# Issuing an attention head's turn, the next head's scores and the previous head's weighing between the same two projection blocks

## The reference

```
proj = rmsnorm(x) @ w_in
A: 4 heads, each with two score maps:  p = softmax(q1 k1) - lam * softmax(q2 k2);  out = p @ v   (v 128 wide)
B: a gated mixing over chunks of 128 tokens
C: 8 heads of 64, three dilated windows combined by their log sums;  out = p @ v
x + (sum over branches of sigmoid(gate) * (y_branch @ w_branch)) @ w_out
```

## Time and profile before

| | |
|---|---|
| runs | median 1844.72 us (1844.07 to 1848.36, 3 runs) |
| profiled execution | span 1845.3 us |
| TensorE | busy 96%, 84% of the chain that ended last |
| VectorE, ScalarE, GpSimd | busy 70%, 56%, 1% |
| granted TensorE clock | mean 0.994 |
| first layer's slots 20 to 57 | about 79.7 to 205.6 us of the span |
| second layer's | about 358.5 to 484.5 us |

### The profile page before, as it was taken

How to read it: one execution, slowest core, us unless ns; L and a number is a source line. 1 busy time by engine, 2 the same in 40 slices (tenths; PEclk the granted TensorE clock), 3 DMA queues, 4 the chain that set the end, 5 groups by cost and what they waited for, 6 DMA issues and landing times.

```text
span 1845.3 us, 46473 instructions
## 1 busy us (share of the span) xinstructions
PE 1776.4 (96%) x18048; PEld 1707.5 (93%) x18048; DVE 1291.2 (70%) x2618; ACT 1034.4 (56%) x2049; POOL 23.5 (1%) x20
## 2 busy tenths in 40 slices
PE   7999999999999999999999999999989988899998
PEld 7999999999998999988899999999987877799998
DVE  6788687788686765587566764676558786657764
ACT  7656656656655555556456554555445844255553
POOL 0110000110000000000000000000000000000000
PEclk9999999999999999999999999999999999999999
DMA  7555555555564555533235555555562320036663
GB/s 247 158 190 172 161 194 178 160 161 159 158 193 128 182 180 178 165 120 97 66 98 170 174 176 176 163 178 180 178 212 92 106 79 4 4 115 193 190 189 123
DMA packets 76990, 279.07 MB, mean 151 GB/s; under 512 B 9008, under 2 KB 10416, under 8 KB 76336
## 3 DMA queue, kind: packets, MB, share of 16 engines
q1 hardware_dynamic: 76848, 277.03, 47.4%
HBM read 274.90 MB, written 1.05 MB: 150 GB/s over the span
## 4 chain that ended last, share of the span: by engine, by line
PE 84%; DVE 9%; ACT 4%; issue 2%; DMA 1%; SPq 0%; DVEq 0%; ACTq 0%
PE psum L410 24%; PE psum L411 23%; PE psum L412 23%; DVE weights_low L375 3%; ACT weights_high L367 2%; PE psum L2991 1%; DMA weight_ring<-weights_in 1%; PE psum L733 1%; PE psum L2968 1%; PE psum L754 1%; PE psum L2985 1%; PE psum L562 1%; PE psum L2575 1%; DVE arena L2974 0%; PE psum L745 0%
## 5 line engine op out<-in xcount | busy, mean ns | idle before, releaser
L375 DVE TENSOR_TENSOR weights_low<-weight_ring,weights_high 128x512 fp32r<-128x512 f32 x984 | 666.5, 697 | 413.3 <-ACT weights_high L367 400.2
L367 ACT ACTIVATE weights_high<-weight_ring 128x512 fp32r<-128x512 f32 x984 | 603.5, 628 | 509.0 <-PE psum L412 506.0
L410 PE MATMUL psum<-ffn_normed_high,weights_high 128*128 128x272 f32 x1056 | 303.9, 288 | 3.4 <-DVE weights_low L375 2.1
L412 PE MATMUL psum<-ffn_normed_high,weights_low 128*128 128x272 f32 x1056 | 302.6, 287 | 0.0
L411 PE MATMUL psum<-ffn_normed_low,weights_high 128*128 128x272 f32 x1056 | 302.6, 287 | 0.0
L410 PE MATMUL psum<-first_normed_high,weights_high 128*128 128x256 f32 x1024 | 293.2, 286 | 5.2 <-DVE weights_low L375 4.6
L411 PE MATMUL psum<-first_normed_low,weights_high 128*128 128x256 f32 x1024 | 285.1, 278 | 0.0
L412 PE MATMUL psum<-first_normed_high,weights_low 128*128 128x256 f32 x1024 | 285.1, 278 | 0.0
L410 PEld LDWEIGHTS psum<-first_normed_high,weights_high 128*128 128x128 f32 x1024 | 193.1, 189 | 14.9 <-DVE weights_low L375 7.2
L410 PEld LDWEIGHTS psum<-ffn_normed_high,weights_high 128*128 128x128 f32 x1056 | 198.9, 188 | 5.9 <-issue 5.7
L411 PEld LDWEIGHTS psum<-ffn_normed_low,weights_high 128*128 128x128 f32 x1056 | 198.9, 188 | 0.1
(11 more groups left out here) (490 smaller groups left out, 3726.3 us busy)
## 6 DMA issues: line engine op xcount, KB each, us to landing
weight_ring<-weights_in SPq DMA_DIRECT2D x507, 512.0 KB, 3.5
arena<-first_in SPq DMA_DIRECT2D x1, 2112.0 KB, 11.0
consts<-const_in SPq DMA_DIRECT2D x1, 1895.0 KB, 7.6
arena<-vec_in SPq DMA_DIRECT2D x1, 1536.0 KB, 8.9
arena<-vec_in SPq DMA_DIRECT2D x1, 1152.0 KB, 5.6
residual<-x_in SPq DMA_DIRECT2D x2, 544.0 KB, 5.2
normed<-arena SPq DMA_DIRECT2D x64, 16.0 KB
out<-normed SPq DMA_DIRECT2D x4, 256.0 KB, 2.3
```

Of the source, the lines that this page charges most:

```text
L367: nc.scalar.activation(WH[:, n % SPLIT, half], W[:, n % RING, half], ACT.Copy).then_inc(weights_high, 1)
L375: nc.vector.tensor_tensor(WL[:, n % SPLIT, half], W[:, n % RING, half], WH[:, n % SPLIT, half].bitcast(F32), ALU.subtract).then_inc(weight ...
L410: nc.tensor.matmul(psum, WH[:, s, cols], high, start=start, stop=False)
L412: return nc.tensor.matmul(psum, WL[:, s, cols], high, start=False, stop=stop)
```

## The change

Scores now stand three slots ahead of a head's turn, which is the slot of the turn of the head before it. Weighing stands in the slot of the next head's turn; for the last head it stays one behind. Maximum and taking move with them, the exponential moves to t-2 and normalising to t-1. Within a slot the order on PE is scores, turn, weighing, and on DVE maximum, taking, normalising, as before. No operation is added or left out.

```diff
+        SCORES_AT = {i - 3: head for i, head in HEADS_AT.items()}
+        WEIGH_AT = {i + 3 if i + 3 in HEADS_AT else i + 1: head for i, head in HEADS_AT.items()}
...
-                if i + 4 in HEADS_AT:
-                    head_scores(*HEADS_AT[i + 4])
+                if i in SCORES_AT:
+                    head_scores(*SCORES_AT[i])
                 if i in HEADS_AT:
                     head_turn(*HEADS_AT[i])
-                if i - 1 in HEADS_AT:
-                    head_weigh(*HEADS_AT[i - 1])
+                if i in WEIGH_AT:
+                    head_weigh(*WEIGH_AT[i])
...
-                if i + 3 in HEADS_AT:
-                    kind, h = HEADS_AT[i + 3]
+                if i + 2 in HEADS_AT:
+                    kind, h = HEADS_AT[i + 2]
                     act_exp(act, attn[kind, l], h)
...
-                if i + 4 in HEADS_AT:
-                    kind, h = HEADS_AT[i + 4]
+                if i in SCORES_AT:
+                    kind, h = SCORES_AT[i]
                     dve_masked_max(dve, attn[kind, l], h, mask_c if kind == "C" else mask_a)
-                if i - 1 in HEADS_AT:
-                    kind, h = HEADS_AT[i - 1]
+                if i in WEIGH_AT:
+                    kind, h = WEIGH_AT[i]
                     if kind == "A":
                         dve_take_head(dve, attn[kind, l], h, YS[:, 0:4])
...
-                if i + 2 in HEADS_AT:
-                    kind, h = HEADS_AT[i + 2]
+                if i + 1 in HEADS_AT:
+                    kind, h = HEADS_AT[i + 1]
                     dve_normalise(dve, attn[kind, l], h, NEG_LAM[:, l:l + 1])
```

## The result

The changed kernel takes 1856.37 us (median of 6 runs, 1853.33 to 1859.54) where the kernel before takes 1845.39 beside it (6 runs, 1841.98 to 1850.02): a ratio of 1.0061, with a 95% interval from 1.0047 to 1.0075. It is slower by about 11 us; forecast were 12.

A forecast was written before the change was run, and what follows sets the result against it. TensorE was taken as the bound, with 84% of the chain. Turn stalls of 14.6 us, less 2.3 for block 29's wait and 0.4 for seams, gave +11.9: median 1857 us, 8-in-10 range 1849 to 1862.

The forecast's parts named there:

- DVE's and ACT's lateness: Ahead of head turns: exponentials and normalising, moved one block later, end late, so TensorE stalls 7.30 us per layer.
- the rope pair ahead of C1 and C3: DVE slots 25 and 31: a rope pair of 1.51 us delays normalising, so each turn stalls 0.92 us.
- GpSimd's 0.9 at C1 and 0.7 at C2: DVE's normalising there may meet GpSimd's rope product: 0.9 and 0.7 us more stall, each 0 to 1.3.
- ACT's branch part at A1: Slot 48: ACT's high part of branch C adds 0.94 us of work, so A1's turn stalls 1.03 us.
- The wait at block 29: Behind C2's turn, low weights late on DVE: the whole 1.15 us goes, 2.3 us for two layers.
- Seams: Between small work and projection blocks: scores followed by turns save 0.35 us per layer, net 0.2, or 0.4 in all.
- the 0.15 given back: Slots 19 and 33: scores C0/C1 and weighing C2/C3 lose their company, costing 0.15 us per layer (0 to 0.2).
- Rival 1: Only the large stalls, at C1, C3, A1 and A3, are real: +5.1 us, 1850; chance 0.18.
- Rival 2: DVE's normalising is never late, only block 29's wait and seams count: 1842 or 1841 us; chance 0.07.
- Rival 3: Late turns delay DVE's weight parts, so projection blocks wait too: +17 to +19 us, 1863; chance 0.09.
- Rival 4: TensorE's clock falls to 1.2 GHz for one block at each of 24 turns: +65 us, 1920; chance 0.01.
- clock 1.00: A listed sign of the forecast: TensorE's granted clock stays at 1.00, that is, does not fall.

The follow-up runs named there:

- e2: Changed kernel with weighing and taking put back one slot behind the turn, so only scores, maximum, exponential and normalising move: 1859.14 us, 1.0057 to the kernel before.
- e3: Changed kernel with each turn, and ACT's copy of it, one slot later, restoring the distance from scores to turn: 1848.50 us, 1.0015 to the kernel before.
- e5: Changed kernel with DVE's normalising issued ahead of the rope pair in its slot: 1854.61 us, 1.0056 to the kernel before.
- e7: Changed kernel with GpSimd's cosine product of rope pairs 5 and 6 cut to 8 of 256 columns: 1849.21 us, one run.
- e6: Changed kernel with ACT's high part of branch C in slot 50 instead of 48, DVE's low part in 51 instead of 49: 1858.89 us, one run.
- e1: Kernel before with only weighing and taking moved to the slot of the next head's turn: 1846.67 us, 0.9990 to the kernel before.
- e4: The changed kernel run once more, unaltered: 1856.67 us, 1.0053 to the kernel before.
- e8: Changed kernel with two scratch fills added on DVE ahead of C1's normalising, to lengthen TensorE's wait: 1862.11 us, one run.

## Why the prediction was right, step by step

**DVE's and ACT's lateness.** This was the core of the forecast, and it held: 7.30 per layer forecast, 7.74 and 8.11 measured. The waits view has TensorE waiting in both stretches for nothing but normalising ahead of a turn; e2 puts four fifths of these waits on the moved scores alone (6.45 and 6.18), and e3 shows them gone when the distance is given back. The terms one by one: the rope pair ahead of C1 and C3 (.92 each) is shown by e5 and measured at .95 in e7; GpSimd's 0.9 at C1 and 0.7 at C2 measured 0.95 to 1.05 and 0.7 to 0.9 (e7 against the changed kernel), at C1 by the meeting with normalising that I had forecast, at C2 by one with the weight splits or the rope pair that stand ahead of it, so that term was right in size more than in place; ACT's branch part at A1 is shown by e6, forecast 1.03, measured 0.97 and 1.17; A3 is 0.15 longer than the sum of its parts, A0 and A2 between 0.1 less and 0.1 more. C5 waits for nothing; C7, for which I had nothing too, waits 0.07. The rule of the Trainium skill (SBUF — State Buffer, "SBUF: two separate sides") that the loser at the port pair waits for the whole instruction fits C1's rows: DVE's operation started at 100.14 with 1.20 of the product to run, took 1.48 less 0.42, that is 1.06, longer than elsewhere, and ended 0.28 behind the product. That the cost then stays in the kernel, and only changes the operation that pays, is what e5 adds.

**What was removed.** The wait at block 29 is gone, 1.15 and 1.18 of it, as said.

**Seams.** The net gain was mis-sized. Groups less waits are 22.39 and 22.34 in the changed kernel, and 24.09 and 24.05 less the 1.15 and 1.18 are 22.94 and 22.87 before: 0.55 and 0.53 per layer, with 12 groups fewer, where I took 0.2. Two terms of my sum were off. "0 to 0.1 each", of which I took the middle, 0.35 in all: scores and a turn cost 1.06 and 0.34 apart (last matmul of a block to the second of the next, less two spacings) and 1.31 to 1.34 together less the wait, so 0.06 to 0.09 is saved at each of the seven, about 0.5. And the 0.15 given back is next to nothing: slots 19 and 20 together cost 2.85 before and after, slots 33 and 35 only 0.03 more. A turn and weighing together save 0.02 at most (e1: 1.33, where 0.34 and 1.01 stood apart). The miss is 0.7 us in two layers.

**The sum.** Layer one: +7.74 −1.15 −0.55 = +6.04, and the stretch grew by 7.39; the 1.35 more are the blocks: 1.5 for the fallen clock less 0.2 for two blocks fewer at the slower spacing. Layer two: +8.11 −1.18 −0.53 = +6.40, less 0.80 in the blocks, gives the 5.60 measured. e4, without a fall, has +12.3 over both, against +11.9 forecast. The runs say +11, and +9.2 for e4. So the total came nearer than its terms: the waits were 1.25 us longer in two layers than forecast and the clock, at nothing in my sum, cost 1.5 more; the seams gave 0.7 more than forecast, and the rest is the spacing of matmuls and code that the change does not touch. That 12 met 11 so closely is in part luck; that the waits of twelve heads came out head by head is not. That the profiled span itself grew only from 1845.3 to 1852.6 is outside the stretches, where that execution was 5.7 us quicker than the one before.

**The rivals.** Rival 1 (small stalls not real) falls: C0, C4 and GpSimd's parts stand in all four profiled layers of the changed kernel. Rival 2 (normalising never late) falls. Rival 3 (weights late behind late turns) did not happen here, but e3 shows that it is near: it comes when DVE's pieces are packed closer in slots 28 to 30. Rival 4 was wrong as put and right in a corner: I asked whether turns, with little else on TensorE, would lower the clock, and gave it 24 turns and 65 us. What lowers it is the idle wait of C1, at most one turn per layer, for 1.4 to 1.6 us, or 2.6 once where the wait was 2.7. My line "clock 1.00" under what would show it is refuted in layer one. I had counted C1's 1.82 of standing still in DVE's terms, and not asked what TensorE's clock makes of it.

## What to carry to other kernels

When a chain over several engines is squeezed by one step, measure from the mark at which the in-order engines are free, and add everything that stands ahead of the piece in its new slot, GpSimd's product included, whichever of DVE's operations it meets. Grouping small work on TensorE saves a twentieth of a microsecond per group here, and only where scores meet a turn, while a chain that comes late pays in full each time. A wait of 2 us on TensorE can cost more than its length, because the next block can run at half clock. Dummies hold the clock but don't take the wait away; distance does. No variant here was shown faster than the kernel before.

## What the runs showed of the chip that I had not expected

**The clock falls behind short waits, near 2 us, and not always.** C1's wait in layers one and two against the clock behind it: changed kernel 2.01 (fell), 1.91 (not); e2 2.01 (fell), 1.81 (fell); e4 1.89, 1.90 (neither); e6 1.91, 1.81 (neither); e8 2.69, 2.80 (both fell). At 2.0 and more it fell in 4 of 4, at 1.8 to 1.9 in 1 of 6. The cost, by the matmuls that stood 0.21 apart instead of 0.11, was 1.4 to 1.6 us, and 2.6 in e8's layer one, where the clock fell during the wait and stood at 0.50 for 6.8 us. Falls also stand outside the changed code, in the kernel before too (clock 0.66 over 815 to 820 us and over 887 to 892 us), so they are part of what differs between executions. Why 1.81 fell in e2 and 1.91 did not elsewhere stays open.

**The spacing of the same matmuls has two values at one clock.** Between two groups of small work, projection matmuls of 256 columns follow each other at 113.4 ns or at 117.8, all at a granted clock of 1.00, and nearly always the value holds until the next group. Of the 40 blocks of a layer's stretch 11 stand at the slower one in the kernel before, in the changed kernel 9 in layer one and 4 in layer two, at 0.1 us per block. It explains layer two's −0.80 (7 blocks fewer, 0.7) and, with 18 and 20 blocks, most of e1's +1.23 and +0.81. No run here tells what chooses between them; it makes up to 1 us per layer between kernels, layers and executions of one kernel, and is a reason why e1's gain could not be seen.
